# RWKV-7 chunks on TensorE: chunk parity in place of the head on the partition halves, 128x128 transposes, products on four 64x64 tiles

## The reference, cut to what matters

```python
def step(state, inp):                      # state 64 x 64 per head, 512 steps
    r_t, w_t, k_t, v_t, a_t, b_t = inp
    sa = jnp.einsum('bhij,bhj->bhi', state, a_t)
    state = (state * w_t[:, :, None, :] + sa[..., None] * b_t[:, :, None, :]
             + v_t[..., None] * k_t[:, :, None, :])
    return state, jnp.einsum('bhij,bhj->bhi', state, r_t)
```

## Time and profile before

| | before |
|---|---|
| median of three runs | 3297.48 us |
| profiled execution, time | 3298.23 us |
| profiled execution, span | 3296.4 us |
| PE busy | 3227.4 us (98%) |
| DVE busy | 1772.7 us (54%) |
| ACT busy | 1247.7 us (38%) |
| POOL busy | 193.2 us (6%) |
| mean granted TensorE clock | 0.994 of 2.4 GHz |

### The profile page before, as it was taken

How to read it: one execution, slowest core, us unless ns; L and a number is a source line. 1 busy time by engine, 2 the same in 40 slices (tenths; PEclk the granted TensorE clock), 3 DMA queues, 4 the chain that set the end, 5 groups by cost and what they waited for, 6 DMA issues and landing times. The chain is left out here.

```text
span 3296.4 us, 52723 instructions
## 1 busy us (share of the span) xinstructions
PE 3227.4 (98%) x22179; PEld 2659.2 (81%) x22179; DVE 1772.7 (54%) x2970; ACT 1247.7 (38%) x1967; POOL 193.2 (6%) x156
## 2 busy tenths in 40 slices
PE   7999999999999999999999999999999999999999
PEld 6877777778888878767788888888888888888887
DVE  5235555555555545364347777433656556655832
ACT  4123343433333332242325666323344344443421
POOL 1000000001001101100001011010000000000000
PEclk9999999999999999999999999999999999999999
DMA  7423333322213135242342213443332233322452
GB/s 232 118 78 87 92 90 92 97 87 68 67 54 93 48 123 163 70 134 74 96 125 77 58 37 92 144 143 106 85 88 90 79 94 90 100 89 80 160 144 86
DMA packets 492528, 324.30 MB, mean 98 GB/s; under 512 B 27130, under 2 KB 448605, under 8 KB 491782
## 3 DMA queue, kind: packets, MB, share of 16 engines
q1 hardware_dynamic: 492294, 320.94, 33.2%
HBM read 276.05 MB, written 44.85 MB: 97 GB/s over the span
## 5 line engine op out<-in xcount | busy, mean ns | idle before, releaser
L534 PE MATMUL PS<-XH,WHT 128*128 128x512 f32 (+1 forms) x2224 | 898.3, 404 | 10.8 <-DVE AR L2000 4.9
L522 DVE TENSOR_TENSOR WLT<-AR,WHT 128x1024 fp32r<-128x1024 f32 (+1 forms) x430 | 527.5, 1232 | 662.9 <-ACT WHT L516 662.5
L536 PE MATMUL PS<-XH,WLT 128*128 128x512 f32 (+1 forms) x2224 | 872.6, 392 | 0.0
L516 ACT ACTIVATE WHT<-AR 128x1024 fp32r<-128x1024 f32 (+1 forms) x430 | 446.8, 1042 | 649.5 <-PE PS L536 482.6
L535 PE MATMUL PS<-XL,WHT 128*128 128x512 f32 (+1 forms) x1712 | 672.8, 393 | 0.0
L534 PEld LDWEIGHTS PS<-XH,WHT 128*128 128x128 f32 (+1 forms) x2224 | 417.9, 188 | 114.4 <-issue 10.8
L536 PEld LDWEIGHTS PS<-XH,WLT 128*128 128x128 f32 (+1 forms) x2224 | 418.0, 188 | 96.3
L535 PE MATMUL PS<-ARR,WHT 128*128 128x512 f32 x1024 | 404.5, 395 | 0.0
L535 PEld LDWEIGHTS PS<-XL,WHT 128*128 128x128 f32 (+1 forms) x1712 | 322.1, 188 | 70.9 <-issue 4.6
L535 PEld LDWEIGHTS PS<-ARR,WHT 128*128 128x128 f32 x1024 | 192.4, 188 | 40.3 <-issue 0.2
L534 PE MATMUL PS<-XL,WHT 128*128 128x512 f32 x512 | 203.3, 397 | 0.1
(11 more groups left out here) (487 smaller groups left out, 5366.1 us busy)
## 6 DMA issues: line engine op xcount, KB each, us to landing
AR<-b_w_in SPq DMA_DIRECT2D x128, 512.0 KB, 4.0
AR<-w_in SPq DMA_DIRECT2D x122, 512.0 KB, 3.9
AR<-a_w_in SPq DMA_DIRECT2D x48, 512.0 KB, 4.2
AR<-w_out SPq DMA_DIRECT2D x32, 512.0 KB, 4.5
AR<-a_w_out SPq DMA_DIRECT2D x32, 512.0 KB, 4.0
AR<-b_w_out SPq DMA_DIRECT2D x32, 512.0 KB, 4.2
proj_scratch<-AR SPq DMA_DIRECT2D x33, 256.0 KB, 2.0
AR<-a_w_kv_up SPq DMA_DIRECT2D x32, 256.0 KB, 3.5
```

The costliest lines, as they stand in the source:

```text
L516: self.nc.scalar.activation(self.shaped(self.high, n), self.shaped(self.raw, n), ACT.Copy).then_inc(self.s_high, 1)
L522: self.nc.vector.tensor_tensor(self.shaped(self.low, n), self.shaped(self.raw, n), f32(self.shaped(self.high, n)), ALU.subtract).then_inc( ...
L534: mm(out, wh, xh[k0 + c], start=(start and c == 0), stop=False)
L536: last = mm(out, wl, xh[k0 + c], start=False, stop=(stop and c == nk - 1))
```

## The change

- Token-major arrays now have the chunk's parity on the partition halves: half p holds the even (p = 0) or odd (p = 1) chunks, and slot 2*c2+e holds chunk 2*c2+p of head e.
- `token_major` is four 128x128 transposes (a block of two chunks and two heads) in place of 16 products.
- Products from feature-major to token-major arrays (`gram`, `lower`) read the rows of head e and write the partitions of parity p; products the other way (`increments`, `outputs`, `queries_solved`) read the rows of parity p and write the partitions of head e. They are issued over all four (e, p), that is over all four 64x64 quarters of the array, and the two row halves write into different banks. Products within token-major arrays (levels, `value_scores`, `solved`) and the state's stay on the diagonal; their count is the same.
- Since the result lies in two banks, VectorE's `gti`, `hb`, `qt`, `t0a` become two instructions of half the columns each, and ScalarE's copy of the output too.
- `outputs` moves ahead of `queries_solved` and `state(i, 1)`; the four groups of transposes, `gram`, `bonus_sums` and `lower` are placed anew between the state products. On VectorE `rates` moves behind `bare_states`, the order of the list between the updates changes, the projection tile is taken out of PSUM ahead of the gram, the weight split of step 3 moves behind the first level of the next pair, the low half of the output behind the gram. On ScalarE the copy of the output moves behind the first level.

```diff
             def token_major(i, x, bank, src, ready, free):
                 N.wait(pe, i, ready, free)
-                N.did(each(range(NCH), lambda c, e: mm(B[bank][rows(e), tok(c)], src[rows(e), tok(c)], C("eye")[rows(e), :], start=True, stop=True)), "pe", "t" + x)
+                for c2 in range(TB):
+                    last = nc.tensor.transpose(B[bank][:, blk(c2)], src[:, blk(c2)], C("ident"))
+                N.did(last, "pe", "t" + x)
...
+            def crossed(cs, f):
+
+                for c2 in cs:
+                    for p, e in ((0, 0), (1, 1), (0, 1), (1, 0)):
+                        last = f(c2, e, p)
                 return last
...
+                for c2 in (2 * j, 2 * j + 1):
+                    for n in range(2):
+                        last = []
+                        for p, e in ((0, 0), (1, 1), (1, 0), (0, 1)):
+                            c, at = 2 * c2 + p, 4 * CH * (c2 % 2) + 2 * CH * n
+                            last.append(mm(B[2 + e][rows(p), at:at + 2 * CH], (SQN, LW)[n][rows(e), tok(c)], AR[rows(e), :, tok(c)], start=True, stop=True))
...
+                G.did(crossed(range(TB), lambda c2, e, p: mm(B[e][rows(p), tok(c2)], AR[rows(e), 0, tok(2 * c2 + p)], SQN[rows(e), tok(2 * c2 + p)], start=True, stop=True)), "pe", "lm")
...
             def increments(i):
...
+                S.wait(pe, i, "act.ptc0", "act.ptc1", f"dve.ta1{NL - 1}")
+                S.did(crossed(range(TB), lambda c2, e, p: mm(B[2 + p][rows(e), tok(c2)], P1TA[rows(p), 2 * c2 + e, 1, :], TOK[rows(p), B_, 2 * c2 + e, :], start=True, stop=True)), "pe", "gt")
+                for c2 in range(TB):
+                    crossed((c2,), lambda c2, e, p: mm(B[p][rows(e), tok(c2)], TOK[rows(p), K_, 2 * c2 + e, :], TOK[rows(p), V_, 2 * c2 + e, :], start=True, stop=False))
+                    last = crossed((c2,), lambda c2, e, p: mm(B[p][rows(e), tok(c2)], TOK[rows(p), B_, 2 * c2 + e, :], P1TA[rows(p), 2 * c2 + e, 0, :], start=False, stop=True))
+                S.did(last, "pe", "h")
...
                 increments(i)
+                outputs(i)
                 queries_solved(i)
                 state(i, 1)
-                outputs(i)
+                if more:
+                    values_turned(i + 1)
                 state(i, 2)
                 if more:
-                    values_turned(i + 1)
+                    bs_turned(i + 1)
                 state(i, 3)
                 piece(i, 7)
                 state(i, 4)
                 if more:
-                    bs_turned(i + 1)
+                    ks_turned(i + 1)
                 state(i, 5)
                 if more:
-                    ks_turned(i + 1)
+                    as_turned(i + 1)
                 state(i, 6)
                 if more:
-                    as_turned(i + 1)
+                    gram(i + 1, 0)
+                    bonus_sums(i + 1)
                 from_state(i)
                 if more:
-                    bonus_sums(i + 1)
-                    for g in range(4):
-                        gram(i + 1, g)
                     lower(i + 1)
+                    gram(i + 1, 1)
...
                 S.wait(dve, i, "pe.h")
...
+                for p in halves:
+                    S.did(TTn(HB[:, p::2, :], B[p][:, 0:T // 2].rearrange("p (c f) -> p c f", f=CH), WC2[i % 2][:, p::2].unsqueeze(2).broadcast_to([P, TB, CH]), ALU.mult), "dve", f"hb{p}")
...
+                state_inputs(i)
+                bare_states(i)
                 if more:
                     rates(i + 1)
-                state_inputs(i)
+                state(i, 1)
                 if more:
                     decayed_rates(i + 1)
-                bare_states(i)
+                state(i, 2)
                 if tail:
                     out_bonus(i - 1)
-                state(i, 1)
+                state(i, 3)
                 if tail:
                     out_gated(i - 1)
                 if more:
                     scaled_keys(i + 1)
-                state(i, 2)
-                if more:
                     decayed_keys(i + 1)
-                state(i, 3)
-                if more:
                     removals(i + 1)
+                state_queries(i)
                 state(i, 4)
-                state_queries(i)
                 if more:
                     queries(i + 1)
                 state(i, 5)
                 if more:
                     bonus(i + 1)
                 state(i, 6)
+                evac(tile(i, 1))
+                if more:
+                    grams(i + 1, 0)
+                    first_level(i + 1)
+                    grams(i + 1, 1)
+                    second_side(i + 1)
+                    put_bonus(i + 1)
```

More of the change, by code:

```diff
@@ L1486, in sums @@
                     S.wait(pe, i, f"act.xc{h}{l}")
[L1488 to L1493 removed]
+                    for c in range(HC):
+                        for n in range(2) if l < NL - 1 else (1,):
+                            for p in halves:
+                                x, t = X[rows(p), HC * h + c, :], TT[rows(p), h, 1, c, :]
+                                last = mm(B[2 + h][rows(p), tok(HC * n + c)], (t, x)[n], (x, t)[n], start=True, stop=True)
+                    S.did(last, "pe", f"t{h}{l}")
             def value_scores(i):
@@ new lines, in increments, with outputs @@
+                S.did(last, "pe", "h")
+            def outputs(i):
+                E.wait(pe, i - 1, "dve.ve", "dve.yn")
+                if i + 1 < NPAIR:
+                    N.wait(pe, i + 1, "dve.nmax")
+                else:
+                    S.wait(pe, i, "dve.hb0")
+                for c2 in range(TB):
+                    crossed((c2,), lambda c2, e, p: mm(out_bank(i, p)[rows(e), tok(2 * c2 + p)], P1TA[rows(p), 2 * c2 + e, 0, :], GB[rows(p), 2 * c2 + e, 1, :], start=(c2 == 0), stop=False))
+                    last = crossed((c2,), lambda c2, e, p: mm(out_bank(i, p)[rows(e), tok(2 * c2 + p)], TOK[rows(p), V_, 2 * c2 + e, :], GB[rows(p), 2 * c2 + e, 3, :], start=False, stop=False))
+                S.did(last, "pe", "y")
@@ L1547, in from_state @@
-                S.did(each(range(1, NCH), one), "pe", "yf")
+                S.wait(pe, i, "dve.qt0", "dve.qt1", f"dve.su{NCH - 2}")
+                for c in range(1, NCH):
+                    for e in heads:
+                        state = HB[rows(e), 0, :] if c == 1 else ST[rows(e), c, :]
+                        last = mm(out_bank(i, c % 2)[rows(e), tok(c)], state, QT[rows(e), tok(c)], start=False, stop=(c >= NCH - 2))
+                S.did(last, "pe", "yf")
             def centred(i):
@@ L2032, in _ @@
             put_bonus(0)
-            gram(0)
+            grams(0, 0)
+            first_level(0)
+            grams(0, 1)
+            second_side(0)
             ahead(6)
@@ L2045, in _ @@
                     level(i, 1, l)
+                    if l == 1 and tail:
+                        split(i - 1, 3)
                     if l in (1, 2, 4):
@@ L2091, in _ @@
                 state(i, 6)
+                evac(tile(i, 1))
[5 more added lines that the diff above has]
+                    put_bonus(i + 1)
                 if tail:
                     low(i - 1)
-                split(i, 3)
-                evac(tile(i, 1))
-                if more:
-                    put_bonus(i + 1)
-                    gram(i + 1)
+                if not more:
+                    split(i, 3)
             i = NPAIR - 1
```

156 lines of the change are left out of this document (71 added, 85 removed).

## The result

The changed kernel takes 3254.03 us (median of 4 runs, 3251.47 to 3255.11) against 3296.85 us for the kernel before on the same chip (4 runs, 3294.13 to 3299.18): a ratio of 0.9869 [0.9852, 0.9886], 42.8 us less. The forecast was 3255 us, in a range of 3246 to 3284. The sum met the time to 1 us; its terms didn't all do so, and two misses, one of about 7 us each way, cancel.

What follows compares the result with a forecast made beforehand. TensorE's issued instructions were taken to bound the kernel. Six full pairs at -5.9 us (-35.4), pair 6 -2.7, pair 7 -2.0 and -3.0 ahead of the loop gave -43: 3297.5 to 3254.5, forecast 3255 us, range 3246 to 3284.

Steps and rivals of the forecast that it cites:

- The bound: Whole mixer: TensorE's instructions set a pair's cost; its busy time should fall by 40 us, the stretch by 43.
- 64 columns on four quarters: Seven groups of 16 products in a full pair run side by side, 0.93 to 0.49 us each: minus 3.1 us.
- Rival A: Loads within a row half go one after another: 64-column groups gain nothing, the gram does; 3278 us, chance 0.22.
- B: A row half serves one quarter at a time; only transposes and order count: 3293.5 us, chance 0.12.
- C: A quarter's load waits for the matmul in its row half's other quarter; groups take 1.75 us: 3345 us, chance 0.08.
- Gram: A full pair's 64 gram instructions of 128 columns run side by side, 3.69 to 1.9 us: minus 1.8 us.
- Turned arrays and the state products between them: Full pair: four transposed arrays go from 0.93 to 0.68 us each, minus 1.0; state products' stalls add 0.3.
- Idle time at `hb`: Between queries and first state product: TensorE's wait goes with `outputs` placed in between, minus 0.3 us per full pair.
- Full pair: Pairs 0 to 5: all terms together minus 5.9 us a pair, minus 35.4 for six.
- Pair 6: Shorter increments, queries, gram and lower, less 0.7 us more waiting before the last pair: minus 2.7 us.
- Pair 7: Last pair's tail: 9.55 us falls to 7.5 by shorter groups and state steps of 0.7 us, minus 2.0.
- The two ends: Ahead of the loop two turned arrays, gram and lower give minus 3.0 us; behind the mixer nothing gives the gain back.

Runs made afterwards that it cites:

- experiments 4 and 5: The projection tile's evacuation ahead of the mixed input at level 3: undone in the changed kernel, 3258.44 us; made alone in the kernel before, 3290.77 us.
- experiment 1: Changed kernel with each group's products reordered, the two diagonal quarters first for all chunks, then the two off the diagonal: 3268.11 us, 0.991.
- t_shift: Changed kernel with its 128x128 transposes written as identity products, plus 64 more transposes (128 TensorE instructions) ahead of the loop: 3271.13 us, 0.9917.
- shift: Changed kernel with 64 more transposes (128 TensorE instructions) ahead of the loop: 3268.39 us, one execution.
- t_products: Changed kernel with each 128x128 transpose written as a float32 product with the identity, 8 instructions per array in place of 4: 3276.24 us, 0.9934.

## Why the forecast met the time, point by point

**The bound.** Right: over the mixer TensorE's busy time fell by 46.7 us (526.97 to 480.23, forecast 40) and the stretch by 43.1 (forecast 43).

**64 columns on four quarters.** Forecast 0.93 to 0.49 us a group, seven groups, minus 3.1. Measured in pair 2: 6.68 us before and 3.31 after, minus 3.4, at 0.47 a group. Rival A (loads one after another in a row half), B and C are refuted: a group of theirs would have taken 0.97, 0.93 and 1.75 us. (The price of a load in A and C, 0.12 us, is busy time of loads that overlap, at a mean length of 191 ns; no run measures a load alone.) The Trainium skill, TensorEngine Tiling (Array Packing), "Instruction Overhead", gives the 60 cycles an instruction from which I had estimated 0.80 us for a group; the trace disagrees, it measures 0.47.

**Gram.** Forecast 3.69 to 1.9; measured 2.03, minus 1.7 in place of 1.8. Each half is followed by a pause before the next full-array product (901.06 to 901.24 is without a start), of which the sum knew nothing.

**Turned arrays and the state products between them.** The arrays: forecast 0.68, measured 0.55 to 0.62, minus 1.5 in place of 1.0. But the way into the transposes, which I had booked with the array, appears in the state product ahead of them, 0.26 us (895.14 to 895.40, the same ahead of a transpose) where it was 0.12 to 0.17, and B's transposes do wait for `bt`: 894.07 to 894.59, 0.25 more (the view calls it "issue", but VectorE's `bt` ends at 894.48). The state products' share went from 0.92 to 1.62 us, +0.7 where the sum had +0.3. The waits for the state updates, from which the sum had its 0.3, don't occur: in full pairs no state product has an idle row that VectorE ended. Together minus 0.8, forecast minus 0.7.

**Idle time at `hb`.** Gone, as forecast. Full pair: minus 6.17 in pair 2 and minus 5.99 as the mean of six, forecast 5.9. Pairs 4 and 5, whose mask stands behind the gated tile's evacuation, are 1.3 us longer than the others; they were 0.9 longer before.

**Solver stretches.** Missed: the sum has no term for them. The move of `evac(tile(i, 0))`, which the whole diff has (neither the cut one nor the list of changes ahead of the prediction shows it) and the prediction leaves out, gave the 6.8 us, as experiments 4 and 5 show: 5.3 of waiting and some 1.6 of clock. The waits had rows in the view of the kernel before (6.7 us, above), of which the move took 4.9; they would have priced most of it. The clock's part no row of waits shows.

**Pair 6.** Forecast minus 3.4 in the tail and plus 0.7 at the next level. The level is right (31.91 to 32.54 and 32.87; it starts behind VectorE's long instruction, as forecast). The tail is not: 17.91 to 17.45 and 19.04. Of the 3 us missed in the first profile, the stop for instructions is 1.7 and the low clock 1.5: behind 1126.0 the gram half takes 2.0 us instead of 1.0, and the turned array and state product ahead of it 0.6 more. In the second the stop is 2.0 and the clock stays low for 10 us instead of 3.4.

```profile
1115.43:1124.00 8.57, 5.47 (x217) 4.54 (x216) 6.48 (x15) 4.42 (x8) 0.00 (x0) 1.00 0.64 216
1124.00:1132.89 8.89, 7.52 (x143) 5.64 (x143) 5.88 (x14) 1.53 (x3) 0.00 (x0) 0.81 0.37 120
```

Before, the clock stood at 1.00 in this tail with TensorE busy for 17.41 of 17.92 us; now it is busy for 5.47 of 8.57 us, and behind that the clock falls from its level of 2.4 GHz to that of 1.2. This isn't chance: in the 20 us from the start of this tail the clock was 1.00 in all four profiles with the old layout and 0.66 to 0.91 in all ten with the new one. Shorter work on TensorE has bared waits for VectorE's list (1.6 us at K's array, 0.8 at a state product) and added the stop for instructions; which of these idle times the clock fell for isn't separated.

**Pair 7.** Forecast minus 2.0; measured +0.5 and +0.1 (10.51 to 11.05 and 10.65). Three things went otherwise, and one was miscounted: my 7.5 us held `from_state`, the 9.55 beside it did not; like for like the forecast was minus 3.0. TensorE in order of time in the kernel after:

```profile
1167.69 0.35 PE L1536 MATMUL PS<-AR 64*64 64x64 f32 x8 [0.64 <-DVE RES L1975]
...
1170.80 0.33 PE L1551 MATMUL PS<-RES 64*64 64x64 f32 x4 [0.39 <-DVE RES L1986]
1171.66 0.33 PE L1551 MATMUL PS<-RES 64*64 64x64 f32 x4 [0.52 <-DVE RES L1986]
1173.11 0.33 PE L1551 MATMUL PS<-RES 64*64 64x64 f32 x4 [1.12 <-DVE RES L1986]
...
1174.79 1.76 PE L1559 MATMUL PS<-AR,RES 64*64 64x64 f32 x28 [0.47 <-DVE RES L1986]
```

In the last pair `outputs` writes to bank 0, which holds `h`, and so waits for `hb0`; in full pairs it follows `increments` at once. And the chain of state products is not at 0.7 us a step throughout: one step takes 1.45 us, since VectorE has `yz` and `qt` in its list between two updates:

```profile
1171.33 0.28 DVE L1986 SCALAR_TENSOR_TENSOR RES<-PS,RES 128x64 f32<-128x64 f32 x1
1171.52 0.68 DVE L2007 TENSOR_TENSOR AR<-AR 128x512 f32<-128x512 f32 x1
1172.12 0.75 DVE L1980 TENSOR_TENSOR AR<-PS,STG 128x256 f32<-128x256 f32 x2
1172.78 0.27 DVE L1986 SCALAR_TENSOR_TENSOR RES<-PS,RES 128x64 f32<-128x64 f32 x1
```

With 1.0 for `outputs` and `queries_solved` with that wait, 1.8 for the chain (5.41 in place of 3.65) and 0.7 for `from_state` at the low clock (1.69 in place of 0.96) the 3.5 us to the measured tail are accounted for. Before, `outputs` stood between the first two state products and covered such VectorE instructions.

**The two ends.** Ahead of the loop minus 3.2 against 3.0, where the profiles have the clock's fall in common (39.56 to 36.32), and 1.7 against the profile before that is without it. "Nothing gives it back" behind the mixer looked wrong in the first pair of profiles (10.13 to 12.01 us); the second pair shows that the kernel before has 11.71 there as well. No loss is shown.

**The balance.** A gain that was missed: 6.8 in the solver. Losses that were missed: about 5.8 to 7.3 in pairs 6 and 7 (forecast minus 4.7, measured +1.1 to +2.6). The forecast was right in its mechanism and in the price of a full pair; that it met the time to 1 us is luck. Of the shares, experiments bear out these: another order of the quarters lengthens the full tails by 14.3 us, products in place of transposes by 10.1, and undoing the evacuation's place the solver stretches by 5.3. The gain of four quarters over two (5 us a pair) is read from the rows alone, and no run undid the new place of `outputs`.

## What to carry to other kernels

Lay products of 64 rows by 64 columns so that neighbours in the list use all four quarters of TensorE: here it halved such groups, and the two orders tried within a round of four made no difference. Before pricing the main edit, take every line that the diff moves in another engine's list and look for its row among the waits: here one such move was 5 to 7 us of the gain of 43. Count what the shortened engine covered (the last pairs, where no projection is left), and look for waits called "issue" inside a list of products: if there are any, where the instructions' blocks begin is a cost of some us that another edit can move about.

## What the runs showed of the hardware

- Four quarters take a round of four float32 products of 64 columns (8 instructions) every 0.117 us at the high clock: 32 in 0.47 us, 14.6 ns each, as fast per quarter (58 ns) as when two were in use, so the loads add nothing.
- TensorE's starts do not keep strictly to its list. In the rows above, two instructions of the gram (900.16) start between the first two and the last two of a state product (900.20), and in experiment 1 later products pass earlier ones whose quarters are busy.
- The supply of instructions can stop TensorE. In dense small products gaps of 1.0 to 3.2 us from start to start, without any wait, go and come when 128 instructions are put ahead of the loop. After each of them, in every profile that has one, TensorE starts again 1.2 to 1.5 us after the end of a 16 KB fetch, also in the two gaps of about 3 us in pair 6 of t_shift and shift, which begin 0.8 to 1.0 us ahead of their fetch. (The "issue" row at pair 7's first level, 1.1 us before and 1.4 after, is another matter: it ends with VectorE's instruction of 2.2 us.) The Trainium skill, Runtime: NRT & Kernel Launch, "Instruction fetch mechanics", calls the crossing of such a boundary mostly hidden. The kernel before agrees in all full pairs, at 29 ns an instruction, and the kernel after in all but pair 6; t_products and shift, where the boundaries fall elsewhere among the instructions, disagree in six and in five of the six full pairs. Not settled: why the fetch comes late in pair 6, in a stretch with heavy DMA traffic; no run took that traffic away.
- The granted clock behind the last tail differs between two executions of the same program (1.00 against 0.84 and 0.87 in two stretches), while the mixer takes 546.8 us in both, since in the other profile the clock fell ahead of the loop. What decides it stays open.
